# A hybrid encoder block on eight cores: the first stage issued from one ordered list with other piece sizes, and a fourth buffer for the convolution weights

## The reference

```python
u = rms_norm(h, g_mix)                       # h: 16 meta tokens, then x (4 x 4096 x 1024)
z = u @ w_in                                 # conv value | conv gate | pool | gate A | gate B
gates = sigmoid(z[..., c3:] + b_gate)
a = z[..., :c1] * sigmoid(z[..., c1:c2])     # GLU
a = depthwise_conv31(a) + b_dw
y_conv = silu(layer_norm(a)) @ w_conv_out
m = concat_g(window_mean_g(p) - p), p = z[..., c2:c3], windows 2, 4, 8, 16
y_pool = (einsum(m, w_pool) * pool_scale) @ w_pool_out
h = h + (gates[:D] * y_conv + gates[D:] * y_pool) @ w_o
v = rms_norm(h, g_ffn)
h = h + (silu(v @ w_ffn_gate) * (v @ w_ffn_up)) @ w_ffn_down
out = rms_norm(h, g_final)[meta tokens dropped]
```

## Time and profile before

| | |
|---|---|
| time, median of the runs | 1008.63 us |
| lowest run | 1006.67 us |
| the profiled execution, its own time | 1007.67 us |
| its span on the slowest core (core 3) | 1006.1 us |
| spans of the eight cores | 998.7 to 1006.1 us |
| PE busy | 966.2 us, 96% |
| VectorE, ScalarE, GpSimd busy | 426.8, 289.2, 169.7 us |

### The profile page before, as it was taken

The page is one execution under the profiler, slowest core; times in us unless marked ns, Lnnn a source line. Parts: engine busy times, 40 slices in busy tenths (PEclk is TensorE's granted clock), DMA queues, the critical chain, the costliest instruction groups (busy, mean ns, idle before and its releaser), DMA issues.

```text
span 1006.1 us, 14695 instructions; the slowest of 8 cores (998.7 to 1006.1 us)
## 1 busy us (share of the span) xinstructions
PE 966.2 (96%) x5176; PEld 472.1 (47%) x5176; DVE 426.8 (42%) x622; ACT 289.2 (29%) x479; POOL 169.7 (17%) x224
## 2 busy tenths in 40 slices
PE   3899999997999999999999999999999999999996
PEld 1645555552434444444444444444444444444485
DVE  4556689833596432333466312112211211242454
ACT  2653134344765112211344211111111111121121
POOL 3141212120780000000464011110000000000000
PEclk9999999997999999999999999999999999999999
DMA  9705797876393222222967265543222004222122
GB/s 211 226 3 85 167 219 185 215 196 132 49 204 85 32 32 32 32 32 49 329 250 167 43 100 100 83 80 60 40 42 42 11 1 160 93 84 84 83 85 84
DMA packets 41158, 105.81 MB, mean 105 GB/s; under 512 B 5760, under 2 KB 14208, under 8 KB 38528
## 3 DMA queue, kind: packets, MB, share of 16 engines
q0 software_dynamic: 21472, 51.46, 28.6%
q1 hardware_dynamic: 19616, 53.42, 15.9%
HBM read 115.80 MB, written 21.04 MB: 136 GB/s over the span
## 4 chain that ended last, share of the span: by engine, by line
PE 92%; DMA 3%; DVE 2%; ACT 1%; issue 1%; POOL 1%; DVEq 0%; ACTq 0%; POOLq 0%
PE ps L364 90%; PE ps L678 2%; DMA xb<-xp 1%; DMA cw<-cw 1%; DVE uT L391 1%; DVE sqx L378 1%; DMA wslot<-w_pool_out 1%; POOL d L378 0%; ACT sqx L375 0%; ACT ps L375 0%; DVE h2b L391 0%; POOL wslot L194 0%; ACT cell L375 0%; ACT sq L375 0%; ACT weff L375 0%
## 5 line engine op out<-in xcount | busy, mean ns | idle before, releaser
L364 PE MATMUL ps<-vT,wslot 128*128 128x512 bf16 x1408 | 304.4, 379 | 0.0
L364 PE MATMUL ps<-uT,wslot 128*128 128x416 bf16 (+6 forms) x1536 | 295.1, 349 | 6.6 <-DVE uT L391 5.2
L364 PEld LDWEIGHTS ps<-uT,wslot 128*128 128x128 bf16 x1536 | 149.4, 99 | 149.6 <-issue 22.0
L364 PEld LDWEIGHTS ps<-vT,wslot 128*128 128x128 bf16 x1408 | 137.7, 98 | 167.0 <-issue 1.6
L378 DVE TENSOR_TENSOR fT<-ps,sgf 128x512 bf16<-128x512 f32 x88 | 60.7, 691 | 228.8 <-PE ps L364 228.8
L364 PE MATMUL ps<-fT,wfd 128*128 128x512 bf16 (+1 forms) x880 | 153.2, 336 | 0.0
L375 ACT ACTIVATE sgf<-ps 128x512 f32<-128x512 f32 x88 | 52.5, 597 | 241.6 <-PE ps L364 234.3
L364 PEld LDWEIGHTS ps<-fT,wfd 128*128 128x128 bf16 x880 | 86.1, 98 | 67.8 <-issue 1.7
L364 PE MATMUL ps<-cell,wslot 128*128 128x512 bf16 x512 | 114.8, 379 | 0.0
L391 DVE SCALAR_TENSOR_TENSOR zt<-zt,ps 128x512 f32<-128x512 f32 x64 | 43.8, 687 | 104.1 <-PE ps L364 103.3
L375 ACT ACTIVATE zt<-ps,hb 128x512 f32<-128x512 f32 x64 | 43.8, 686 | 139.4 <-PE ps L364 137.7
(11 more groups left out here) (77 smaller groups left out, 605.8 us busy)
## 6 DMA issues: line engine op xcount, KB each, us to landing
rep<-ad SPq DMA_DIRECT2D x128, 129.5 KB, 5.2
wslot<-w_in POOLq DMA_DIRECT2D x40, 256.0 KB, 7.2
h1d<-h1b SPq DMA_DIRECT2D x4, 2048.0 KB, 8.9
h2b<-h1d SPq DMA_DIRECT2D x4, 2048.0 KB, 12.5
h1b<-xr SPq DMA_DIRECT2D x3, 2048.0 KB, 17.7
out<-h2b SPq DMA_DIRECT2D x3, 2048.0 KB, 8.3
wslot<-w_ffn_gate POOLq DMA_DIRECT2D x22, 256.0 KB, 4.7
wslot<-w_ffn_up POOLq DMA_DIRECT2D x22, 256.0 KB, 3.6
```

The lines of the kernel that those rows point to most:

```text
L364: S.op(PE, lambda e: e.matmul(out, lhsT=lhsT, rhs=rhs, start=start, stop=stop), [lhsT, rhs], [out], signal=stop if signal is None else signal)
```

## The change

The first stage is issued from one list, `START`, instead of from the calls. Each entry is a step: `qPH` squares channel chunks 2H and 2H+1 of piece P (on VectorE for `q02` and `q03`, otherwise on ScalarE), `aPI` is the I-th of four adds of piece P, all on VectorE, `SP` (a capital S and the piece) the stat with its Ln and Exp, `nPH` four of the eight norms, `tPC` the tile of output chunk C, and `w0` queues the first window sums. The pieces are 256, 256, 256, 416, 448 and 448 tokens instead of 160, 256, 320, 416, 448 and 480. The convolution's weights get a fourth buffer, outside the area of the other three.

```diff
-PIECES = ((0, 160), (160, 256), (416, 320), (736, 416), (1152, 448), (1600, 480))
+PIECES = ((0, 256), (256, 256), (512, 256), (768, 416), (1184, 448), (1632, 448))
+START = """q00 q01 q03 q02 a00 a01 a02 a03 S0 q11 n00 q10 n01 a10 q12 q13 a11 a12 t00 a13 t02 S1 t01 q23 n10 t03
+q21 q22 n11 t04 q20 t12 a21 a20 t15 t05 a22 a23 t10 S2 q33 q30 q31 t11 q32 n20 t13 n21 a30 t14 t16 t06 t21 t22 t23
...
@@
+    cw.append(alloc("cw3", [128, 4, 4, 32], BF16))
@@
-    xoffs = [oM, oM + 160 * 32, oM + 416 * 32, oZ, oZ + 416 * 32, oW]
+    xoffs = [oM, oM + 256 * 32, oM + 512 * 32, oZ, oZ + 416 * 32, oW]
@@
-    cw_sem = [dsem(f"d_cw{i}") for i in range(3)]
+    cw_sem = [dsem(f"d_cw{i}") for i in range(4)]
@@
-    def s1_squares(p):
-        o, n = PIECES[p]
-        x = xb[p]
-        sq = sqx[:, :, o:o + n]
-        if p < 3:
-            act(sq[:, 0:4, :], x[:, 0:4, :], AF.Square)
-            tt(DVE, sq[:, 4:8, :], x[:, 4:8, :], x[:, 4:8, :], ALU.mult)
-            tt(DVE, sq[:, 0:4, :], sq[:, 0:4, :], sq[:, 4:8, :], ALU.add)
...
-        eng = DVE if p == 3 else POOL
...
+    def square(p, h):
+        o, n = PIECES[p]
+        dst, x = sqx[:, 2 * h:2 * h + 2, o:o + n], xb[p][:, 2 * h:2 * h + 2, :]
+        if p == 0 and h >= 2:
+            tt(DVE, dst, x, x, ALU.mult)
+        else:
+            act(dst, x, AF.Square)
+
+    def add_squares(p, i):
+        o, n = PIECES[p]
+        a_, b_, w_ = ((0, 2, 2), (4, 6, 2), (0, 4, 2), (0, 1, 1))[i]
+        dst = sqx[:, a_:a_ + w_, o:o + n]
+        tt(DVE, dst, dst, sqx[:, b_:b_ + w_, o:o + n], ALU.add)
@@
-    s1_squares(0)
-    s1_norm(0)
-    s1_squares(1)
-    tiles((0,), (0, 1))
-    s1_norm(1)
...
+    for t in START.split():
+        k, p, i = t[0], int(t[1]), int(t[2:] or 0)
...
+        elif k == "t":
+            pool_tile(p, i)
+            pump(1)
@@
-        S.dma(POOL, cw_sem[g % 3], cw[g % 3][:].rearrange("p j q m -> p (j q m)"), cw_d.ap()[g])
+        S.dma(POOL, cw_sem[g % 4], cw[g % 4][:].rearrange("p j q m -> p (j q m)"), cw_d.ap()[g])
@@
-            if g + 3 < NG:
-                load_cw(g + 3)
+            if g + 4 < NG:
+                load_cw(g + 4)
@@
-    for g in range(3):
+    for g in range(4):
         load_cw(g)
```

More of the change, by code:

```diff
@@ L34 @@
 NSLOT = 9
-PIECES = ((0, 160), (160, 256), (416, 320), (736, 416), (1152, 448), (1600, 480))
+PIECES = ((0, 256), (256, 256), (512, 256), (768, 416), (1184, 448), (1632, 448))
+START = """q00 q01 q03 q02 a00 a01 a02 a03 S0 q11 n00 q10 n01 a10 q12 q13 a11 a12 t00 a13 t02 S1 t01 q23 n10 t03
+q21 q22 n11 t04 q20 t12 a21 a20 t15 t05 a22 a23 t10 S2 q33 q30 q31 t11 q32 n20 t13 n21 a30 t14 t16 t06 t21 t22 t23
+t26 a31 a32 t07 a33 S3 q43 t24 q42 q40 n30 n31 q41 a40 a41 q53 t25 q51 t17 t27 t20 t30 a42 t31 t32 a43 q52 t33 S4
+a51 q50 n40 n41 a50 t34 t35 t36 t37 a52 a53 t40 t41 t42 S5 t43 t44 n51 n50 w0 t45 t46 t47 t50 t51 t52 t53 t54 t55
+t56 t57"""
 NX = len(PIECES)
@@ L504, in alt, with s1_stat @@
         return ap.rearrange("p (x e) -> p e x", e=2)
-    def s1_squares(p):
+    def square(p, h):
         o, n = PIECES[p]
-        x = xb[p]
-        sq = sqx[:, :, o:o + n]
-        if p < 3:
-            act(sq[:, 0:4, :], x[:, 0:4, :], AF.Square)
-            tt(DVE, sq[:, 4:8, :], x[:, 4:8, :], x[:, 4:8, :], ALU.mult)
-            tt(DVE, sq[:, 0:4, :], sq[:, 0:4, :], sq[:, 4:8, :], ALU.add)
-            tt(DVE, sq[:, 0:2, :], sq[:, 0:2, :], sq[:, 2:4, :], ALU.add)
-            tt(DVE, sq[:, 0, :], sq[:, 0, :], sq[:, 1, :], ALU.add)
-            return
-        eng = DVE if p == 3 else POOL
[L518 to L525, removed]
+        dst, x = sqx[:, 2 * h:2 * h + 2, o:o + n], xb[p][:, 2 * h:2 * h + 2, :]
[8 more added lines that the diff above has]
+        tt(DVE, dst, dst, sqx[:, b_:b_ + w_, o:o + n], ALU.add)
+    def s1_stat(p):
         o, n = PIECES[p]
@@ L530, in s1_norm @@
         act(psum[7][:, 0:n], st, AF.Exp, scale=-0.5)
-        for k in range(KC):
+    def s1_norm(p, h):
+        o, n = PIECES[p]
+        for k in range(4 * h, 4 * h + 4):
             stt(DVE, uT[:, k, :, o // 2:(o + n) // 2], par(xb[p][:, k, :]), pcc(PC_GMIX, k), par(psum[7][:, 0:n]),
@@ L542, in pool_tile @@
             release(f"pool{c}")
[L544 to L547, removed]
     win_done = set()
@@ L584, in windows @@
         return out
-    s1_squares(0)
-    s1_norm(0)
-    s1_squares(1)
-    tiles((0,), (0, 1))
-    s1_norm(1)
[L591 to L614, removed]
+    for t in START.split():
+        k, p, i = t[0], int(t[1]), int(t[2:] or 0)
+        if k == "q":
+            square(p, i)
+        elif k == "a":
+            add_squares(p, i)
+        elif k == "S":
+            s1_stat(p)
+        elif k == "n":
+            s1_norm(p, i)
+        elif k == "t":
+            pool_tile(p, i)
+            pump(1)
+        else:
+            for c in (6, 7):
+                bg.extend(windows(c, 0))
     S.dma(SP, pms, pmask[:], pm_d.ap())
@@ L674, in conv @@
                         o = ps[32 * j:32 * j + 32, :]
-                        lt = cw[g % 3][:, j, q, :]
+                        lt = cw[g % 4][:, j, q, :]
                         x0 = h * TT + 4 * q
```

## The result

The changed kernel takes 990.76 us in the median of four runs (988.96 to 991.02), the kernel before 1007.56 us beside it. Some executions of every version are slow ones, with a lower granted clock on one die and up to 20% more time, and every median in this text leaves them out. The ratio is 0.983, with a 95% interval of 0.981 to 0.985: 1.7% faster, within 2%. The forecast was 994.5 us with a range of 990 to 1001. The direction was right, and the range held, by 0.8 us at its lower end. Span against span, 16.6 us were gained (1006.1 to 989.5) where 13.2 were forecast (1006.1 to 992.9).

A forecast was written before the change was run, and what follows sets the result against it. PE bounds the kernel, through its waits and low clock on the slowest core. From 1006.1 us of span, 8.0 for the fourth buffer and 5.2 for the first stage leave 992.9; with 1.6 around it 994.5 us, range 990 to 1001.

The forecast's parts named there:

- the case that I gave 0.62: Whole kernel: both parts work as forecast and the time is 992.5 to 997 us.
- more than forecast: First stage: landing by 10.1, no norm waits, full clock from 24 us; 991.5 us; chance 0.10, another 0.05 below 988.5.
- The fourth buffer: Convolutions: PE's wait for weights before group 13 goes; 8.0 us gained on the slowest core.
- core 3's 9.7 us: Core 3, conv(5) to conv(7): 30.8 us becomes 21.1; only 8.0 count because core 6 becomes slowest.
- No return of the wait at conv(7): conv(7): about 3 us of cover for the rep loads; the rival, a returning wait, 999.5 us, chance 0.08.
- The first stage: From start to the first matmul of the second stage: ends at 86.1 us against 91.3, 5.2 gained.
- the first unknown: Start of the first stage: 0.39 MB more in piece 0 take 3.3 us, landing at 10.9, between 10.1 and 13.6.
- the walk: First stage on core 3, step by step from piece 0's landing through stats, norms and tiles, to 86.1 us.
- the low clock's pace: First stage once PE is dense, from 29.85 us: slow matmuls at the low clock cost 0.3 us.
- stat 3's wait: First stage, piece 3: its adds follow norms ending near 37.7 us, so PE waits 0.4 us.
- ScalarE's queue: First stage: squares stand between a tile and its copy on ScalarE, costing 0.5 us.
- The starved piece: Start: piece 0's last 0.39 MB trickle in behind POOL's pieces; whole gain gone or 1029.5 us; chance 0.04.

The follow-up runs named there:

- e1: The kernel before with the fourth convolution weight buffer alone: 1000.32 us, ratio 0.991.
- e7: The kernel before, three weight buffers, with the slots of the last vg released after conv(5) instead of before: 1001.64 us, ratio 0.993.
- e4: The changed kernel with the old piece sizes, so the list and the fourth buffer: 991.36 us, ratio 0.982.
- e3: The kernel before with the new piece sizes and the fourth buffer, but the old calls instead of the list: 998.18 us, ratio 0.989.
- e5: The changed kernel with the adds of pieces 4 and 5 on GpSimd again: 993.63 us, ratio 0.985.
- e9: The changed kernel with three tiles of piece 0 moved from behind stat 1 to ahead of it: 995.78 us, ratio 0.987.
- e10: The changed kernel with the five tiles behind stat 3 moved ahead of it: 996.24 us, ratio 0.987.
- e6: The changed kernel with piece 0 loaded by two DMAs, in rows of 4 KB instead of 8: 990.62 us, ratio 0.982.

## Why the prediction was right, and where it was off

The range held, but what came is not the case that I gave 0.62 (992.5 to 997 us). It is the last rival, more than forecast, to which I gave 0.10: 991.5 us, against 990.76. Its first condition, a landing at 10.1 or sooner, was met on every core. Its other two were not quite: PE still waits 2.3 us for norms, and it is at full pace from about 27 us, not from 24. The mechanism was right, and one term of the sum was mis-sized.

**The fourth buffer** was right to a tenth: 21.1 us from conv(5) to conv(7), measured 20.98 on core 0 and 21.0 on all cores of e1; 999.7 us for it alone, measured 1000.3. So was the point that not all of core 3's 9.7 us count, since another core takes its place: 8 were forecast, and the longest span went from 1006.1 to 998.8 in e1. I had overlooked core 0, whose span of 1005.9 us and stretch of 28.7 put it at 998.2, beside core 6 at 998.1; the sum doesn't change by it. What I said of the cause was half right. Group 13's load was hardly held by the stores: its buffer is free only when group 10 has been computed, in conv(5), and by then the last store was being issued (223.72 us on core 3). What made it late was mainly the two loads just ahead of it in the queue, as e7 shows.

**No return of the wait at conv(7)**: right. Of the eleven traces with the fourth buffer none has a wait for `rep` there on any core. With three buffers and the later release (e7) one core waits 0.5 us, so the cover is not wide.

**The first stage** gained more than the 5.2 us forecast: 9.7 us by the core that comes last to conv(5) in each kernel (223.75 to 214.04), 9.0 in the mean of the four later cores. The step that failed is the first unknown, the landing of piece 0. I took 10.9 us, the measured starts of its squares are 6.3 to 8.9; the bounds, 10.1 to 13.6, did not hold it either. From there the walk was good: stat 0 to stat 1 was forecast at 8.6 us and is 9.1, stat 1 to the last stat about 41.4 (86.1 less the last stat and 13 tiles of 448 columns gives 65.4 us) and is 41.2. Stat 1 came at 21.0 us instead of 24.0, and the first stage ended at 83.0 (214.04 less the 131.0 us that lie between on core 3 of before) instead of 86.1. Those 3.1 us are nearly all that the forecast was off: 992.9 us of span against 989.5.

Part of the walk's agreement is luck. From stat 1 to stat 2 I had 8.5 us and it took 9.5, because PE was at the low clock's pace until about 27 us (last section), which I had priced at 0.3 us from 29.85 on. The 0.9 us for stat 3's wait and for ScalarE's queue then did not come.

Why was the landing misjudged? I read 0.31 MB in 4 to 6 us as the rate of SP's queue, though the same row says that only 68% of the engines' time was used. At full use it would have been 0.23 MB in a microsecond and a landing at 9.3 us. And the piece ended inside the window, so the number was what was left of it, not what the queue could do. Windows of one microsecond show it. SP's queue (q1) in 3 to 4 and in 4 to 5 us on core 3, kernel before:

```profile
q1 hardware_dynamic: 48, 0.25, 92.5%
q1 hardware_dynamic: 51, 0.19, 88.2%
```

and on core 0, after:

```profile
q1 hardware_dynamic: 31, 0.25, 82.9%
q1 hardware_dynamic: 39, 0.32, 106.2%
```

Both are later cores. In 3 to 4 us they move the same, with rows of 5 KB and of 8 KB; in 4 to 5 us the smaller piece is running out, and the larger one goes on at 0.28 to 0.34 MB on the later cores. So the 0.39 MB more took 1.1 us on the later cores and 1.4 on the others, in the means of four, where I had put 3.3. The rest of the miss is the start: I added to 7.6 us, the latest of the eight cores, and the four later ones had 7.1 in the mean. In 4 to 6 us of the changed kernel on core 0, q1 and q0:

```profile
q1 hardware_dynamic: 76, 0.54, 96.8%
q0 software_dynamic: 1, 0.00, 3.8%
```

The rule of the Trainium skill that I weighed (DMA: Bandwidth & Descriptors, "Queues, rings and completion order": the engines go round between queues that have work) would, as I applied it, have put the landing at 11.5 us, further off. The two queues did not share the engines by halves here: POOL's queue, whose first load is issued at 1.6 us in both kernels, had moved one packet by 6 us on core 0. Its first packets come at 4.0 to 5.5 us in the kernel before and at 5.0 to 6.5 in the changed one, by core, about when SP's piece runs out. Whether it had nothing to move until then or had to wait for its turn, no row shows. The starved piece, the rival on the other side, falls with the same row.

**Why the stage gained** I had put on the first piece feeding more work and on density in general. The runs are clearer than my argument: with the old sizes and the list the time is the same within 1.1 us (e4), with the new sizes and the old calls 7.4 us or more are missing (e3), of which the adds on GpSimd explain some 3 (e5), and carrying three or five tiles over one stat costs over 5 us (e9, e10). So the term that my sum treated as given, hardly a wait behind any stat, was the gain itself. PE's windows over the whole stage, core 3 before and core 0 after (from:to, length, PE busy, count), say how it comes about:

```profile
0.00:91.29 91.29, 69.88 (x398) 1.00 0.56 134
0.00:83.03 83.03, 67.35 (x398) 1.00 0.60 147
```

Of the 8.3 us between these two cores 5.7 are waits, 2.1 of them for `sqx` and 2.9 for norms, and 2.5 are a shorter busy time for the same columns, which fits more matmuls at full clock (the granted clock can't show it here, see the last section).

**Small terms.** The adds moved to VectorE end in time, as forecast; on GpSimd they would have cost 2.9 to 3.8 us (e5), which I had not priced. The forecast had 0.5 us for ScalarE's queue. On cores 2, 5 and 7 of the changed kernel stat 1 waits 0.6 us behind a ScalarE copy; after that no core has such a wait in the first stage.

## What to carry to other kernels

On an engine that runs in order, a reduction whose result comes back through other engines should have work queued behind it that needs nothing from it, for as long as the way round takes; count the tiles between each such step and its first user before changing any size. When a small load is late, look first at what stands ahead of it in its queue: releasing two large loads a little later brought 7.4 us, a new buffer 8.9. And a rate is read only from a window in which the transfer neither starts nor ends, and compared only between cores that are in the same position.

## What the runs showed of the hardware

At the start, when all eight cores load, neighbouring cores do not get the same. In 3 to 4 us SP's queue moved 0.25 to 0.26 MB on the later cores of the kernel before and 0.35 to 0.40 on the others, and 0.25 to 0.27 against 0.38 to 0.42 in the changed kernel. What the cores of such a pair share, no run shows. Beside that, larger rows moved no more in this window: with 5 KB before and 8 KB after it is the same, and with rows of 4 KB (e6) it is 0.29 to 0.30 and 0.39 to 0.41 MB. The extra 0.39 MB cost 1.1 to 1.4 us of landing; the same bytes in two loads of 4 KB rows cost 0.7 to 1.2 more, and whether the rows or the second load did that is not separated.

The load of group 13's convolution weights, 128 KB, took 5.2 to 9.2 us by core to land behind two of 256 KB on GpSimd's queue and 2.8 to 4.3 us without them.

Of the clock at the start the profile's column tells nothing. On core 0 of the changed kernel, columns as in the earlier trace rows but of PE alone:

```profile
24.00:26.00 2.00, 2.00 (x11) 1.00 0.99 301
28.00:30.00 2.00, 2.00 (x21) 1.00 1.01 203
```

Both say 1.00, yet 11 matmuls of 256 columns fall into the first 2 us and 21 into the second (a matmul that reaches over an edge is counted too). PE is busy throughout in both. Half the pace is what 1.2 GHz against 2.4 would give, so I take the first for the low clock. Where no earlier record of a change exists, the pace of equal matmuls is the better witness.
